# A new order for the router and the first expert gather, with five spare TensorE products between their parts

## The reference, cut to what matters

```python
logits = t @ router_w + router_b              # t = rms_norm(x, norm_ffn), 32 experts
top_v, top_i = lax.top_k(logits, 4)
gates = softmax(top_v)
# for each expert e: the rows t[tok] of the tokens that chose it
hu = t[tok] @ w_up[e] + b_up[e]               # 1024 -> 2048
act = (clip(hu[:, 1::2]) + 1) * gate * sigmoid(1.702 * gate)   # gate = min(hu[:, ::2], 7)
y[tok] += gates * (act @ w_down[e] + b_down[e])
```

## Time and profile before

| | |
|---|---|
| Time, median of 3 executions | 1325.25 us (1323.56 to 1326.96) |
| The profiled execution: its own time, its span | 1327.2 us, 1325.6 us |
| Busy share of the span: PE, PEld, DVE, ACT, POOL | 95%, 43%, 31%, 18%, 7% |
| Mean granted TensorE clock | 0.977 of full |
| DMA, mean over the span | 350 GB/s, 463.58 MB |
| Expert section | from 383.55 us of the span to its end |

### The profile page before, as it was taken

The page is one execution under the profiler, slowest core; times in us unless marked ns, Lnnn a source line. Parts: engine busy times, 40 slices in busy tenths (PEclk is TensorE's granted clock), DMA queues, the critical chain, the costliest instruction groups (busy, mean ns, idle before and its releaser), DMA issues.

```text
span 1325.6 us, 19940 instructions
## 1 busy us (share of the span) xinstructions
PE 1253.5 (95%) x7878; PEld 571.4 (43%) x7878; DVE 406.7 (31%) x921; ACT 240.6 (18%) x401; POOL 92.3 (7%) x167
## 2 busy tenths in 40 slices
PE   8999999799989999999999999999999999999996
PEld 6777766587433333333333333333333333333332
DVE  4721434542732212222222132222213222222224
ACT  3222333323211011111111011011101101011103
POOL 6101141152000000000000000000000000000000
PEclk9999998889979999999999999999999999999999
DMA  9644699100769999999999999999999999999993
GB/s 325 228 131 114 219 387 357 27 20 6 301 213 382 427 428 430 428 428 428 428 429 429 429 427 429 428 429 429 428 429 429 428 429 430 428 429 429 428 428 141
DMA packets 66105, 463.58 MB, mean 350 GB/s; under 512 B 16654, under 2 KB 16782, under 8 KB 41478
## 3 DMA queue, kind: packets, MB, share of 16 engines
q1 hardware_dynamic: 62808, 452.22, 83.3%
q0 software_dynamic: 3200, 10.49, 2.1%
q10 hardware_dynamic: 46, 0.18, 0.0%
HBM read 459.15 MB, written 3.70 MB: 349 GB/s over the span
## 4 chain that ended last, share of the span: by engine, by line
PE 47%; DMA 23%; issue 1%; DVE 0%; SPq 0%; ACT 0%; POOLq 0%; POOL 0%; DVEq 0%; ACTq 0%
PE bank L2051 28%; DMA ring<-in_w_up 20%; PE bank L2068 6%; PE bank L2020 4%; PE bank L1999 4%; DMA hoT<-in_w_down 2%; PE bank L2003 1%; PE bank L2024 1%; PE bank L2040 1%; PE bank L2095 1%; PE bank L2076 0%; PE bank L2106 0%; SPq L750 0%; ACT work L2158 0%; PE bank L2009 0%
## 5 line engine op out<-in xcount | busy, mean ns | idle before, releaser
L2051 PE MATMUL bank<-ring,work 128*64 128x512 f32 x1536 | 339.9, 597 | 14.6 <-DMA ring<-in_w_up 14.6
L2051 PEld LDWEIGHTS bank<-ring,work 128*64 128x64 f32 x1536 | 109.3, 137 | 243.3 <-issue 231.1
L2068 PE MATMUL bank<-ring,work 128*64 128x512 f32 x768 | 173.0, 596 | 7.5 <-ACT work L2158 5.5
L410 PE MATMUL bank<-hoT,ring 128*128 128x288 f32 x448 | 113.0, 407 | 1.1 <-ACT hoT L445 0.8
L2051 PE MATMUL bank<-hoT,work 128*64 128x512 f32 x256 | 112.9, 594 | 0.0
L2051 PE MATMUL bank<-work 128*64 128x512 f32 x256 | 112.9, 594 | 0.0
L2250 DVE TENSOR_SCALAR work<-bank 128x512 f32<-128x512 f32 x32 | 21.9, 684 | 257.8 <-PE bank L2051 257.8
L2068 PEld LDWEIGHTS bank<-ring,work 128*64 128x64 f32 x768 | 55.7, 137 | 103.1 <-issue 99.2
L410 PEld LDWEIGHTS bank<-hoT,ring 128*128 128x128 f32 x448 | 83.5, 190 | 23.2 <-ACT hoT L445 0.9
L2142 ACT ACTIVATE work<-bank 128x1024 f32<-128x1024 f32 x16 | 16.4, 1023 | 383.8 <-PE bank L2003 383.8
L2212 DVE TENSOR_TENSOR X<-X,bank 128x512 f32<-128x512 f32 x64 | 44.0, 687 | 108.9 <-PE bank L2020 108.9
(11 more groups left out here) (391 smaller groups left out, 1312.9 us busy)
## 6 DMA issues: line engine op xcount, KB each, us to landing
ring<-in_w_up SPq DMA_DIRECT2D x96, 2048.0 KB, 24.6
ring<-in_w_down SPq DMA_DIRECT2D x48, 2048.0 KB, 26.9
work<-in_w_up SPq DMA_DIRECT2D x16, 2048.0 KB, 25.7
hoT<-in_w_up SPq DMA_DIRECT2D x16, 2048.0 KB, 30.1
work<-in_w_down SPq DMA_DIRECT2D x8, 2048.0 KB, 25.1
hoT<-in_w_down SPq DMA_DIRECT2D x8, 2048.0 KB, 29.4
ring<-in_w_in SPq DMA_DIRECT2D x7, 2048.0 KB, 16.6
ring<-in_cache_k SPq DMA_DIRECT2D x48, 256.0 KB, 3.1
```

The source lines that it names most:

```text
L410: ins = pe.matmul(bank[0:m, i % 2, 0:T], w[:, k, :], hT[:, k, :], start=k == 0, stop=k == KD - 1)
L2051: ins = pe.matmul(bank[CAP * e:CAP * e + CAP, g, :], xT[:, k, CAP * e:CAP * e + CAP], weight(odd, ch + e, k % 2 * RSLOT + 512 * g), start= ...
L2068: ins = pe.matmul(bank[CAP * e:CAP * e + CAP, 4 + m, :], aT[:, k, CAP * e:CAP * e + CAP], weight(odd, ch + e, k % 4 * D + 512 * m), start= ...
```

## The change

One product with 512 columns whose result nobody reads is a `keep_busy`. One such product is put before and one after the transposes of tile 1, one after the products of L1560 and L1561, and two at the very end of TensorE's block. The logits of tile 1 move ahead of the products of L1560 and L1561 and use bank 3 instead of bank 2, so their wait for `d_Sout` 4 moves down to the last part of the gather. The bank 1 product of tile 1 moves behind the first part of the gather. The gather's last part signals each half by itself, and the copy, the transposes and the copies after them run by halves. Two semaphores are used a second time (`d_Sout` counts to 5, `d_WQ` to 2).

```diff
-        LOGIT_BANK = {2: 5, 0: 3, 1: 2}
+        LOGIT_BANK = {2: 5, 0: 3, 1: 3}
+        s_half_gathered, s_half_copied = d_Sout, d_WQ
@@ TensorE
+                def keep_busy(n, b):
+                    for _ in range(n):
+                        pe.matmul(bank[:, b, :], ident[:], h2[:, 0, 0:512], start=True, stop=True)
@@
                 logits(1, 0)
+                keep_busy(1, 4)
                 turn_row(2, 1)
+                keep_busy(1, 4)
                 pe.wait_ge(s_mk, 2)
                 pe.matmul(bank[:, 4, 0:NE], Uinc, mk[:, 0, :], start=True, stop=True)
...
+                logits(2, 1)
                 for b in (5, 1):
                     pe.matmul(bank[:, b, 0:NE], ones[:], mk[:, 0, :], start=True, stop=False)
                     pe.matmul(bank[:, b, 0:NE], ones[0:ND, :], mk[0:ND, 2, :], start=False, stop=False)
-                pe.wait_ge(d_Sout, 4)
-                logits(2, 1)
+                keep_busy(1, 7)
                 pe.wait_ge(s_mk, 3)
                 pe.matmul(bank[:, 5, 0:NE], Uinc, mk[:, 1, :], start=False, stop=True).then_inc(s_rank, 1)
-                pe.matmul(bank[:, 1, 0:NE], ones[:], mk[:, 1, :], start=False, stop=True).then_inc(s_rank, 1)
                 pe.wait_ge(M["P"], 1)
                 for m in range(2):
                     pe.matmul(bank[:, 6 + m, :], Pm[:, 0:P], h2[:, 0, 512 * m:512 * (m + 1)], start=True, stop=False)
+                pe.matmul(bank[:, 1, 0:NE], ones[:], mk[:, 1, :], start=False, stop=True).then_inc(s_rank, 1)
...
+                pe.wait_ge(d_Sout, 4)
                 pe.wait_ge(M["P"], 2)
-                for m in range(2):
-                    ins = pe.matmul(bank[:, 6 + m, :], Pm[:, P:2 * P], h2[:, 1, 512 * m:512 * (m + 1)], start=False, stop=True)
-                ins.then_inc(M["gathered"], 1)
-                pe.wait_ge(M["x_copied"], 1)
-                for k in range(KD):
-                    ins = pe.transpose(bank[:, 6 + k // 4, (k % 4) * P:(k % 4 + 1) * P], xs[:, k * P:(k + 1) * P], ident[:])
-                    if k % 4 == 3:
-                        ins.then_inc(M["xT_turned"], 1)
+                pe.matmul(bank[:, 6, :], Pm[:, P:2 * P], h2[:, 1, 0:512], start=False, stop=True).then_inc(s_half_gathered, 1)
+                pe.matmul(bank[:, 7, :], Pm[:, P:2 * P], h2[:, 1, 512:D], start=False, stop=True).then_inc(M["gathered"], 1)
+                for q in range(2):
+                    if q == 0:
+                        pe.wait_ge(s_half_copied, 1 + 1)
+                    else:
+                        pe.wait_ge(M["x_copied"], 1)
+                    for k in range(4 * q, 4 * q + 4):
+                        ins = pe.transpose(bank[:, 6 + q, (k % 4) * P:(k % 4 + 1) * P], xs[:, k * P:(k + 1) * P], ident[:])
+                    ins.then_inc(M["xT_turned"], 1)
+                keep_busy(2, 2)
@@ ScalarE
+                act.wait_ge(s_half_gathered, 4 + 1)
+                act.activation(xs[:, 0:512], bank[:, 6, :], ACT.Copy).then_inc(s_half_copied, 1)
                 act.wait_ge(M["gathered"], 1)
-                act.activation(xs, bank[:, 6:8, :].rearrange("p b n -> p (b n)"), ACT.Copy).then_inc(M["x_copied"], 1)
+                act.activation(xs[:, 512:D], bank[:, 7, :], ACT.Copy).then_inc(M["x_copied"], 1)
```

## The result

| | before | after |
|---|---|---|
| Median of 20 executions each | 1324.74 us (1319.79 to 1332.06) | 1321.62 us (1314.50 to 1328.74) |
| Ratio, 95% interval | | 0.9966 (0.9951 to 0.9982) |
| Span of the profiled execution | 1325.6 us | 1321.7 us |
| Its granted clock, mean over the span | 0.977 | 0.981 |

A forecast was written before the change was run, and what follows sets the result against it. The weight stream, started by the first freed buffer, bounds the kernel. Held clock gives 5.55 + 0.8 = 6.35 us, a partial fall 6.35 - 1.7 = 4.65; their middle, 5.5, gives 1319.8 us, range 1316.9 to 1325.0.

The forecast's parts named there:

- What bounds the kernel: Weight loads set the kernel's end; bringing the first use of a buffer (394.03 us) forward moves the stream one for one.
- Rival 3: Stream of weights: the earlier start isn't handed on because something else limits it, end stays 1325.3 us; chance 0.06.
- The router at the high clock: Up to tile 1's logits: with the clock at 2.4 GHz they end at 364.54 against 368.26, 3.72 us earlier.
- The cover behind the logits: Behind tile 1's logits: VectorE's choice (2.04 us) hides eight records and a spare product (1.93 us), unless the clock is low.
- two cases: Router and experts' start: clock held gains 6.35 us; clock falling part of the way loses 1.7, leaving 4.65; together chance 0.64.
- the sign I had named: Router: a granted clock of 0.50 at 361 to 367 us would show the prediction wrong.
- The halves: End of the gather: copies and transposes by halves take 1.9 us from gather's end to the last copy, against 2.89.
- The last two spare products end the block: Block's end: they stand ahead of TensorE's drain; block ends at 375.25 against 380.80, 1.25 us less gain than without them.
- The experts' start: First expert products: a shorter pause ahead saves 0.8 us of the low clock's 2.29 us price there.
- Rival 2: Block's end: the pause no longer lowers the clock, so the whole 2.29 us counts, gain 7.84, 1317.4 us; chance 0.10.
- Rival 1: Router: the clock falls as before at 361 us until 374.8, some 0.7 us gained, 1324.5 us; chance 0.16.
- Rival 4: Block's end: slower, the last two spare products run at the low clock ahead of the drain, 1330.7 us; chance 0.04.

The follow-up runs named there:

- e3: The changed kernel with its two last spare products moved behind the block's end, ahead of TensorE's wait for POOL's clearing: mean 1318.6 us, ratio 0.9950.
- e5: The changed kernel with the two last spare products behind the block's end and the three in the router removed: mean 1319.6 us, ratio 0.9935.
- e4: The changed kernel with each spare product replaced by eight 128-column transposes of about the same duration: mean 1321.2 us, ratio 0.9960.
- e6: e3 with the third spare product directly behind the logits of tile 1 and two small bank 1 products moved into the gather: mean 1316.6 us, ratio 0.9916.
- e8: The changed kernel without its two last spare products, keeping the three in the router: mean 1322.8 us, ratio 0.9968.
- e9: e6 with the two small bank 1 products in TensorE's wait for VectorE's choice instead of the gather: mean 1316.0 us, ratio 0.9916.
- e10: e9 with SyncE's four stores behind chunk 7 also moved into the next block: mean 1318.3 us, ratio 0.9937.
- e7: The changed kernel with only the two last spare products, ahead of the drain, and none of the three in the router: mean 1323.8 us, ratio 0.9972.
- e1: The changed kernel without its five spare products, so only the new order and halves: mean 1323.2 us, ratio 0.9975.
- e2: The kernel before with the five spare products at the same places, nothing reordered: mean 1326.1 us, ratio 0.9988.

## Why the prediction was right, and where its sizes were off

- **What bounds the kernel.** Right, and the firmest part: the first use of a buffer moved by 3.88 us, the span by 3.9, the last load by 3.91. Rival 3 (the earlier start is not handed on) fell in every run.
- **The router at the high clock.** Predicted 364.54 for the end of the logits of tile 1, measured 362.00 + 1.97 = 363.97. The stretch ahead ran a little tighter than my sums, which took full durations where records overlap by 0.1 to 0.2 us each.
- **The cover behind the logits.** The forecast joined two cases; the profile shows the second. The clock fell at about 364.4, the small products and the third spare product took until 367.5, and the triangle product was 2.8 us ahead of before instead of 3.7. Predicted loss 1.7 us, measured 1.3 at the triangle product (367.49 against the mask's 366.21) and some 1.6 in the gather's first part (3.65 against 1.98). I had taken these as either-or; the profile has both, 2.9 us, and the tighter router gave 0.6 of it back. That is why the sum came out at 3.88 and not 4.65. By the sign I had named (a clock of 0.50 at 361 to 367 us) this step was half missed: it was 1.00 up to 364.4 and 0.50 behind.
- **The halves.** Gather's end to ScalarE's end 2.0 us, predicted 1.9, before 2.89.
- **The last two spare products end the block.** Right: 1.1 us behind ScalarE, predicted 1.25. That they cost their time there was in the working (1.25 us); e3 and e5 show what a better place is worth.
- **The experts' start.** Predicted 0.8 us, measured (2.02 + 8.47) - (1.12 + 8.71) = 0.66. (The whole price there, 2.29 us in the prediction, mixes two views of the same records; like with like, 7.02 for 7.09, it is 2.36.) But my reason was a shorter low stretch at an unchanged place; in fact the clock passed the pause high and fell behind it, inside the experts' work. The size is luck. Rival 2 (no fall there at all) was not seen in this kernel; with the two products behind the block's end it is what every profile shows.
- **The time.** 1319.8 us forecast, 1321.62 measured, inside the range of 1316.9 to 1325.0, though not in the forecast case's own 1318.3 to 1321.1; 5.5 us of gain forecast, 4.5 by the ratio, 3.5 by the means, 3.1 by the medians, 3.9 between the two profiles. The 5.5 was the middle of two cases, and the profile shows the worse one, worse than priced. The term mis-sized is the partial fall of the clock: 1.7 us in its case, 2.9 in the profile. That the time fell into the range says little by itself, for a range of 8 us took in rival 1's 1324.5 too, and single executions spread by more; the steps in the timeline are the better evidence.
- **Rival 1** (the clock falls as before, spare products or not) was seen in no profile of the new order with spare work in the router: the logits of tile 1 took 1.97 us in the kernel after, e3, e4, e6, e8, e9 and e10. Without it they took 3.62 us in e5 and e7, but 1.97 in e1, and in the old order with it (e2) 2.55. **Rival 4** (the last two products at the low clock) was not seen. What I had not priced is that all of this varies by execution; three executions and one profile of before didn't show a spread of 12 us.

What stays open: how much of the gain of the kernel after comes from its five spare products and not from the order and the halves, since they raise the clock and cost time in about equal measure; which of the three products in the router earns its place, if any; and whether e9 or e6 is the better. The runs can't tell 1 us.

## What to carry to other kernels

Look for the one moment that everything later follows, here the first freed buffer: what lies behind it took 931.4 to 932.1 us in every profile, so 30 us of trace tell what one execution gained or lost. Whether a variant gains takes many executions: e1's stage was shorter than the changed kernel's, its mean time longer. A product that only keeps the clock up belongs where its engine waits anyway; ahead of a drain or behind a choice that is nearly done it costs its full time, twice that if the clock has fallen (2.08 us against 1.10). And where the granted clock varies by execution, take the mean clock of each execution beside its time: it turned a scatter of 3.4 us into one of 1.5.

## What the runs showed of the hardware that was not expected

The clock did not follow the pauses one by one. In the kernel after it was at 1.00 through 2.7 us without a product and fell to 0.50 afterwards, with TensorE busy. In the router of the same profile it fell at about 364.4 us with no pause ahead of it: TensorE was busy for the whole of 361 to 364.5 us, from 361.6 on with 32-column products alone. In e3, e5, e6, e9 and e10 pauses of 0.9 to 1.8 us and then 0.4 to 0.9 with two products between them left it high. Where in the program it falls differs between executions of kernels that are the same up to there, and with it the start of this stage, 350.94 to 362.26 us.
